# Modulation by rows with an accumulating multiply, and the gates' one-hot matrices in 16 bit with the tokens innermost

## The reference, cut to what matters

```python
c_act = jax.nn.silu(c)                                  # c: 1 x 2048
mod = (c_act @ w_ada[l] + b_ada[l]).reshape(B, 6, 1, D)  # w_ada: 2048 x 12288
shift1, scale1, gate1, shift2, scale2, gate2 = jnp.moveaxis(mod, 1, 0)
h = rmsnorm(x, g_norm_mix[l]) * (1.0 + scale1) + shift1
```

```python
s_half = jnp.einsum('thpd,hpkd->thpk', q, sub_keys)      # 128 keys on each of 2 sides
v_half, i_half = lax.top_k(s_half, K)                    # 16 best of each side, then 16 best pairs
a = jnp.einsum('cd,ced->ce', hc, w_u[ec])
coef = gc * jax.nn.gelu(a)                               # gate times activation
out = jnp.einsum('ce,ced->cd', coef, w_v[ec])
```

## Time and profile before

| | |
|---|---|
| runs, us | 3499.93, 3502.94, 3509.88 (median 3502.94) |
| profiled execution: span from the first to the last instruction, us | 3499.1 |
| around the span: median less span, us | 3.8 |
| busy: PE / DVE / ACT / POOL, us | 3167.9 / 2285.7 / 1244.0 / 155.9 |
| instructions | 51027 |

### The profile page before, as it was taken

The page is one execution under the profiler, slowest core; times in us unless marked ns, Lnnn a source line. Parts: engine busy times, 40 slices in busy tenths (PEclk is TensorE's granted clock), DMA queues, the critical chain, the costliest instruction groups (busy, mean ns, idle before and its releaser), DMA issues. The chain is left out here.

```text
span 3499.1 us, 51027 instructions
## 1 busy us (share of the span) xinstructions
PE 3167.9 (91%) x19812; PEld 2876.9 (82%) x19812; DVE 2285.7 (65%) x2591; ACT 1244.0 (36%) x1305; POOL 155.9 (4%) x240
## 2 busy tenths in 40 slices
PE   6999697998686999876799899999999999999997
PEld 5898476898575899865699899988899889988786
DVE  5674466674466666256637968854887468889844
ACT  4442343442333333032333333334333433333343
POOL 1010001010001100001000000000000000000000
PEclk9999898999898999578899999999999999999998
DMA  7764275764175777102544444455344554444453
GB/s 271 269 223 166 83 255 191 265 233 172 64 257 204 253 276 274 66 1 99 214 158 153 153 150 159 161 183 192 144 156 168 192 180 144 156 150 163 157 193 131
DMA packets 98853, 619.24 MB, mean 177 GB/s; under 512 B 10960, under 2 KB 11088, under 8 KB 35920
## 3 DMA queue, kind: packets, MB, share of 16 engines
q1 hardware_dynamic: 69968, 508.83, 40.7%
q0 software_dynamic: 28800, 109.25, 8.4%
HBM read 615.95 MB, written 2.10 MB: 177 GB/s over the span
## 5 line engine op out<-in xcount | busy, mean ns | idle before, releaser
L1238 DVE TENSOR_TENSOR wl<-ring,wh 128x2048 fp32r<-128x2048 f32 x468 | 1071.5, 2290 | 720.5 <-ACT wh L843 450.9
L843 ACT ACTIVATE wh<-ring 128x2048 fp32r<-128x2048 f32 x468 | 894.8, 1912 | 752.3 <-PE ps L427 305.6
L437 PE MATMUL ps<-hh,wh 128*128 128x256 f32 x3712 | 1068.7, 288 | 32.1 <-DVE wl L1238 23.3
L438 PE MATMUL ps<-hl,wh 128*128 128x256 f32 x3712 | 1057.1, 285 | 0.0
L439 PE MATMUL ps<-hh,wl 128*128 128x256 f32 x3712 | 1057.0, 285 | 0.0
L437 PEld LDWEIGHTS ps<-hh,wh 128*128 128x128 f32 x3712 | 719.5, 194 | 37.5 <-DVE wl L1238 28.2
L438 PEld LDWEIGHTS ps<-hl,wh 128*128 128x128 f32 x3712 | 720.0, 194 | 0.1
L439 PEld LDWEIGHTS ps<-hh,wl 128*128 128x128 f32 x3712 | 719.0, 194 | 0.0
L425 PE MATMUL ps<-wh,hh 128*128 128x512 f32 x864 | 342.8, 397 | 52.7 <-DVE hl L1231 27.7
L426 PE MATMUL ps<-wl,hh 128*128 128x512 f32 x864 | 338.9, 392 | 0.0
L427 PE MATMUL ps<-wh,hl 128*128 128x512 f32 x864 | 338.8, 392 | 0.0
(11 more groups left out here) (235 smaller groups left out, 3004.6 us busy)
## 6 DMA issues: line engine op xcount, KB each, us to landing
ring<-in_stream SPq DMA_DIRECT2D x480, 1024.0 KB, 4.8
aring<-in_ada POOLq DMA_DIRECT2D x192, 512.0 KB, 4.6
X<-in_x SPq DMA_DIRECT2D x1, 2048.0 KB, 11.7
BIG<-in_nbr_bias POOLq DMA_DIRECT2D x2, 1024.0 KB, 5.0
BIG<-in_g_post POOLq DMA_DIRECT2D x2, 1024.0 KB, 5.1
out<-X SPq DMA_DIRECT2D x2, 1024.0 KB, 4.0
BIG<-in_decays POOLq DMA_DIRECT2D x1, 1536.0 KB, 6.8
aring<-in_keys POOLq DMA_DIRECT2D x1, 1024.0 KB, 6.3
```

Of the source, the lines that this page charges most:

```text
L437: mm(o, wh[:, c % 2, w], hh[:, k, :], start=(k == 0), stop=False)
L438: mm(o, wh[:, c % 2, w], hl[:, k, :], start=False, stop=False)
L843: return nc.scalar.activation(o, i, func, **kw)
L1238: return tt(wl[:, c % 2, :], ring[:, c, :], wh[:, c % 2, :].bitcast(F32), ALU.subtract)
```

## The change

- The modulation weights are transposed on the host: each of the 192 units now holds 128 outputs on the partitions and half (1024) of the input rows. DVE does one instruction for a unit, a multiply by the row `crow` that writes its product back into `aring` and its sum into one column of `mod_parts`. `reduce_modulation` and its waits are gone from TensorE. `take_modulation` is two small additions on DVE, done three times in all: after both layers, in the third block after its column projections, and after its output projection.
- `crow` (silu of the condition, repeated on all partitions, 128 x 2048) replaces a column form of 128 x 16. It is loaded with a DMA of its own, issued by SP behind that of `X` and ahead of units 1 to 3 of the ring, and ACT's first `Silu` runs over all of it.
- `acc` is gone; the attention output `OT` takes the place of `PF`/`PF2` chunks, and the decay table is two tables, each with a DMA and a semaphore.
- `hot1`, `hot2`, `index`, the gate parts and an equality matrix are 16 bit with the 8 tokens innermost. The gate has three parts, built once after routing. A copy `iota8` of the key numbers, 8 times repeated, is made on DVE ahead of the routing. `hot2` has two buffers.
- A token's product is 128 x 96 and reads both operands with a step of 8 elements of 16 bit (16 bytes). A batch fills two PSUM banks. `gate_sum` reads 768 values for 512, `gsum` has two buffers, and `gated` runs over contiguous groups of 8 tokens. In a slot DVE now does all of the next batch ahead of the sum of this one.

```diff
-ADA_UNIT = 2 * 512
+ADA_UNIT = DM // 2
+MOD_CUTS = (0, 4 * A_TM2, 4 * A_WO2, 4 * ADA_CG)
...
-        hot1 = sb("hot1", [P, 2, BATCH, KEYS], F32R)
-        hot2 = sb("hot2", [P, BATCH, 2, PART], F32R)
-        gate_parts = sb("gate_parts", [P, 2, SEQ], F32R)
+        hot1 = sb("hot1", [P, 2, KEYS, BATCH], BF16)
+        hot2 = sb("hot2", [P, 2, GATE_PARTS, PART, BATCH], BF16)
+        equal2 = sb("equal2", [P, 2, PART, BATCH], BF16)
+        iota8 = sb("iota8", [P, KEYS, BATCH], BF16)
+        gate_parts = sb("gate_parts", [P, GATE_PARTS, SEQ], BF16)
...
+            sp.dma_start(crow, cond.rearrange("p (a b) -> p a b", a=2)).then_inc(cond_ready, 16)
             for s in range(1, R):
                 sp.dma_start(ring[:, s, :], stream[s]).then_inc(w_ready[s], 16)
...
-                pe.wait_ge(a_used, l * (ADA_LAYER * ADA_H) + ((ADA_TM + ADA_FM) * ADA_H + 2))
-                reduce_modulation(ADA_TM + ADA_FM, 4)
-                pe.wait_ge(mod_done, l * 2 + 1)
...
                 for j in range(BATCH):
-                    last = mm(ps[:, bank, j * 2 * PART:(j + 1) * 2 * PART], hot1[:, b, j, :],
-                              hot2[:, j, :, :].rearrange("p a b -> p (a b)"), start=True, stop=True)
+                    at = (j % 4) * TOKEN_COLS
+                    last = mm(ps[:, bank + j // 4, at:at + GATE_PARTS * PART], hot1[:, b, :, j],
+                              hot2[:, b, :, :, j].rearrange("p a b -> p (a b)"), start=True, stop=True)
...
-            f(csilu[:, :], small_of("cond"), ACT.Silu).then_inc(c_ready, 1)
+            act.wait_ge(cond_ready, 16)
+            f(crow, crow, ACT.Silu).then_inc(c_ready, 1)
...
-            def modulation(cg, h, i):
+            def modulation(cg, h):
                 dve.wait_ge(a_ready[h % 2], cg * 64 + 16 * (h // 2 + 1))
-                for kk in range(2):
...
-                        ins = stt(acc[:, i, :], w, csilu[:, k:k + 1], acc[:, i, :], ALU.mult, ALU.add)
-                    ins.then_inc(a_used if kk else a_step, 1)
+                u = cg * ADA_H + h
+                w = aring[:, h % 2, :]
+                stt(w, w, 1.0, crow[:, h % 2, :], ALU.mult, ALU.mult,
+                    accum_out=mod_parts[:, bass.ds(u, 1)]).then_inc(a_used, 1)
...
+            def take_modulation(part):
...
+                dve.wait_ge(a_used, 2 * end + 2)
+                tt(mod[:, cols], pair[:, :, 0], pair[:, :, 1], ALU.add).then_inc(mod_sum, 1)
+                dve.wait_ge(mod_sum, part + 1)
+                tt(mod[:, cols], mod[:, cols], small_of("b_ada")[:, cols], ALU.add).then_inc(mod_done, 1)
...
+            st(v.tensor_copy(iota8[:, :, :], small_of("iota").unsqueeze(2).to_broadcast([P, KEYS, BATCH])))
...
-            st(tt(gate_parts[:, 1, :], ps[:, 2, 0:SEQ], gate_parts[:, 0, :].bitcast(F32), ALU.subtract))
+            st(tt(gate_left, ps[:, 2, 0:SEQ], gate_parts[:, 0, :], ALU.subtract))
             st.done()
+            st(v.tensor_copy(gate_parts[:, 1, :], gate_left))
+            st.done()
+            st(tt(gate_parts[:, 2, :], gate_left, gate_parts[:, 1, :], ALU.subtract))
...
+                tt(hot1[:, b, :, :], token(index[:, 0, :], t0, KEYS), iota8[:, :, :], ALU.is_equal)
+            def hot_second(q, n, t0, b):
+                tt(equal2[:, b, :, :], token(index[:, 1, :], t0, PART), iota8[:, q * PART:(q + 1) * PART, :],
+                   ALU.is_equal).then_inc(hot_step, 1)
+                dve.wait_ge(hot_step, n + 1)
+                shape = [P, GATE_PARTS, PART, BATCH]
+                tt(hot2[:, b, :, :, :], equal2[:, b, :, :].unsqueeze(1).to_broadcast(shape),
+                   gate_parts[:, :, bass.ds(t0, BATCH)].unsqueeze(2).to_broadcast(shape), ALU.mult).then_inc(hot_done, 1)
...
+                src = ps[:, bank:bank + 2, :].rearrange("p k c -> p (k c)").rearrange("p (t s i) -> p i t s", t=BATCH, s=4)
+                v.tensor_reduce(gsum[b], src[:, :, :, 0:GATE_PARTS], AX, ALU.add).then_inc(sum_step, 1)
...
-                o = act_e[q % 2][:, :, bass.ds(t0, BATCH)].rearrange("p i t -> p t i")
-                tt(o, o, gsum, ALU.mult).then_inc(g_used, 1)
+                o = act_e[q % 2][:, :, bass.ds(t0, BATCH)]
+                tt(o, o, gsum[b], ALU.mult).then_inc(g_used, 1)
...
                 hot_first(t0 + BATCH, (c + 1) % 2)
-                gate_sum(n, bank + c % 2)
-                second_equal(q, t0 + BATCH)
-                gated(q, n, t0)
-                second_low(n + 1, t0 + BATCH)
-                second_high(n + 1, t0 + BATCH)
+                hot_second(q, n + 1, t0 + BATCH, (c + 1) % 2)
+                gate_sum(n, bank + apart * (c % 2), c % 2)
+                gated(q, n, t0, c % 2)
```

More of the change, by code:

```diff
@@ L154, with block @@
 DVE_STEPS, POOL_STEPS = 52, 7
-def block(nc, stream, ada, small, const1, const2, decays, keys, nbr_bias, g_post, g_final, x, out):
+HH = 4480
+WH = HH + 2 * KD * SEQ
+WL = WH + 2 * UNIT
+ACTS = WL + 2 * UNIT
+GATE_PARTS = 3
+TOKEN_COLS = 128
+def block(nc, stream, ada, cond, small, const1, const2, decays, keys, nbr_bias, g_post, g_final, x, out):
     ctx = ExitStack()
@@ L440, in up @@
                 last.then_inc(unit_done, 1)
[L442 to L448, removed]
             def prenorm(i):
@@ L746, in up_quarter @@
                         if q:
-                            batch(i * R + (b0 + c), c % 2, c % 2)
+                            batch(i * R + (b0 + c), c % 2, 2 * (c % 2))
                         up(i + g0, c, i * R + (n0 + c))
@@ L859, in prenorm, with halves, high_operand @@
                           bias=shift(k)).then_inc(ht_done, 1)
-            def high_operand(src):
+            def halves(src):
+                return [src[:, 0:8, :], src[:, 8:16, :]]
+            def high_operand(parts):
                 for half in range(2):
-                    k = slice(half * 8, half * 8 + 8)
-                    f(hh[:, k, :], src[:, k, :], ACT.Copy).then_inc(hh_done, 1)
+                    f(hh[:, half * 8:half * 8 + 8, :], parts[half], ACT.Copy).then_inc(hh_done, 1)
             def high(g, c, free=False):
@@ L1189, in _ @@
             pl.memset(kz, 0.0).then_inc(zeroed, 1)
-            pool.wait_ge(mod_done, 2 * LAYERS + 1)
-            pool.dma_start(area(0, DECAY_W), decays).then_inc(decay_ready, 16)
+            for i in range(2):
+                pool.dma_start(decay3[i].rearrange("p a b -> p (a b)"),
+                               decays[:, i * (DECAY_W // 2):(i + 1) * (DECAY_W // 2)]).then_inc(decay_ready[i], 16)
             pool.wait_ge(nss_done, 1)
@@ L1224, in prenorm, with halves, low_operand @@
                         ts(o, src, scale(k), shift(k), ALU.mult, ALU.add).then_inc(ht_done, 1)
-            def low_operand(src, use):
+            def halves(src):
+                return [src[:, 0:8, :], src[:, 8:16, :]]
+            def low_operand(parts, use):
                 for half in range(2):
@@ L1230, in low_operand @@
                     dve.wait_ge(hh_done, use * 2 + (half + 1))
-                    tt(hl[:, k, :], src[:, k, :], hh[:, k, :].bitcast(F32), ALU.subtract).then_inc(hl_done, 1)
+                    tt(hl[:, k, :], parts[half], hh[:, k, :].bitcast(F32), ALU.subtract).then_inc(hl_done, 1)
                 dve.wait_ge(hl_done, use * 2 + 2)
@@ L1241, in next_low @@
                 low(g + (c + 1) // R, (c + 1) % R).then_inc(lo_done, 1)
-            def modulation(cg, h, i):
+            def modulation(cg, h):
                 dve.wait_ge(a_ready[h % 2], cg * 64 + 16 * (h // 2 + 1))
-                for kk in range(2):
[L1247 to L1256, removed]
-                        ins = stt(acc[:, i, :], w, csilu[:, k:k + 1], acc[:, i, :], ALU.mult, ALU.add)
-                    ins.then_inc(a_used if kk else a_step, 1)
-            def take_modulation(count, n, cols, bank):
-                dve.wait_ge(mod_full, count)
-                tt(mod[:, cols], ps[:, bank, 0:4 * n], small_of("b_ada")[:, cols], ALU.add).then_inc(mod_done, 1)
+                u = cg * ADA_H + h
[3 more added lines that the diff above has]
+            def take_modulation(part):
+                first, end = MOD_CUTS[part], MOD_CUTS[part + 1]
+                cols = slice(first, end)
+                pair = mod_parts[:, 2 * first:2 * end].rearrange("p (a b) -> p a b", b=2)
+                dve.wait_ge(a_used, 2 * end + 2)
+                tt(mod[:, cols], pair[:, :, 0], pair[:, :, 1], ALU.add).then_inc(mod_sum, 1)
+                dve.wait_ge(mod_sum, part + 1)
+                tt(mod[:, cols], mod[:, cols], small_of("b_ada")[:, cols], ALU.add).then_inc(mod_done, 1)
             def rotate(dst, src, tmp, cos, sin, heads, half):
@@ L1455, in _ @@
             st.region(LAYERS * DVE_STEPS)
-            dve.wait_ge(mod_done, 2 * LAYERS)
+            take_modulation(0)
+            dve.wait_ge(mod_done, 1)
             def scales(a, j):
```

132 lines of the change are left out of this document (55 added, 77 removed).

## The result

The changed kernel takes 3536.3 us (median of 4 runs, 3531.3 to 3538.1) against 3502.2 for the kernel before beside it: a ratio of 1.0093, 95% interval 1.0079 to 1.0108. It is slower by 0.9%. Forecast was 3460, so the forecast was wrong, in sign too; what came is the direction of rival 2. The profiled execution spans 3533.0 us, 33.9 more than before's 3499.1.

What follows compares the result with a forecast made beforehand. TensorE was taken to bound the kernel, with DVE as full in V2. Modulation −20.4, gate products −16, DVE's relief −8 and +1.2 sum to −43.2 us, from 3502.9 to 3460 us; range 3420 to 3502.

Steps and rivals of the forecast that it cites:

- rival 2: Gate products on TensorE: the 16-byte step makes each dear, 187 ns, +79 us, 3558 us in all; chance 0.13.
- The modulation: All modulation steps together, from the start through the third block, with DVE's own cost: −20.4 us.
- +1.2 for `iota8` and the steps after routing: DVE's work ahead of routing (`iota8`) and small gate-part steps after it, against a cheaper first batch: +1.2 us.
- Start: Up to the first matmul: the `crow` load adds 2.5 us and the longer Silu 1.7; +4.2 us (0 to 7).
- Layers: Layers 0 and 1: sums over partitions and handshake gone, −13.7 us; 20 transposes faster in each, −3.2 us (0 to −5).
- Third block: Ahead of the compression matmuls: −5.5 us, not the 10.9 the sums take, since POOL's clearing is late next.
- at the output projection: Third block's output projection, DVE's multiply: gain 1.7 us less the new additions' remainder, −1.6 us.
- The gate products: 1024 products on TensorE at 95 ns each instead of 110: −16 us (ends −57 and +79).
- The two ends of that term: Price of a gate product: 54 ns from the stream of columns alone, 187 ns with DVE's 1.7-times step price.
- its relief: DVE's faster gated slots let TensorE keep its pace in V2 and shorten gaps: −8 us (0 to −13).
- That the products keep their price: Gate products stay at 110 to 135 ns because the weight load sets the pace: 3478 to 3503 us; chance 0.17.
- That DVE gains nothing from 16 bit: DVE then bounds V2 with a slot of 6.4 us and the lag stays: 3475 us; chance 0.12.

Runs made afterwards that it cites:

- x4_pairs: Changed kernel with keys innermost, gate-product operands contiguous 16-bit rows, each token's index and gate parts stored twice for VectorE; 3415.1 us, ratio 0.9738 to the kernel before.
- x3_modulation: Changed kernel's modulation with the gate products, one-hot matrices and single gate-sum buffer of the kernel before; 3484.2 us, ratio 0.9936 to the kernel before.
- x2_stepsize: Changed kernel, TensorE's gate operands 4 (U1), 8 (U2), 16 bytes apart with 64 columns (U3), contiguous in V2; sums wrong; 3438.5 us.
- x5_plain: As x4_pairs, but VectorE reads one stored copy of each token's index and gate part, held for the row of keys; 3458.2 us.

## Why the prediction was wrong, step by step

**The modulation: right, within what can be told.** Forecast −20.4 with everything up to the first batch; with +1.2 for `iota8` and the steps after routing, −19.2. Measured at U1's start: −20.7 in the changed kernel, −18.3 in x4_pairs and −15.9 in x3_modulation; by the medians of the runs −22 (−16 to −29) for the modulation alone. Its terms:
- Start: forecast +4.2, measured +5.2 (first row matmul 37.28; before it was at 32.1). The row landed by 15.65, 2.1 us after X before, for 2.5 forecast. The missing term is ACT's table load, 1.28 us, which now comes between landing and Silu; before it stood ahead of the wait (7.66 to 8.94 us).
- Layers: the sums over partitions and their handshake are gone, and the 20 transposes take 2.40 us. In layer 0 the score matmuls behind them, 5.2 us late at the start, come 3.1 us early: −8.3; in layer 1 11.9 early, so −8.8 more. 17.1 against 13.7 + 3.2 = 16.9.
- Third block: TensorE starts the compression at 1393.73 for 1413.51, 7.9 us more in hand than in layer 1. From the end of the column projections to the compression it is 11.4 us before (from 1402.09) and 5.9 after (from 1387.79): −5.5, as forecast, and POOL's clearing is what DVE waits for, as foretold. The other 2.4 us were gained ahead of that step, and no wait was found for them. From the compression to U1 come only 0.9 more (forecast −1.6, at the output projection).
- What these terms can be told from: U1's start varies by 4.8 us among kernels that are the same up to there but for the copy of the key numbers (2049.1 after, 2051.5 in x4_pairs, 2053.9 in x3_modulation, which has no copy and is last). So the +1.2 was not seen, and part of the −20.7 goes with the clock and not with a wait: one less the granted clock, summed over windows of 10 us from 320 to 2050, comes to 155 us in the changed kernel, 161 in x4_pairs, 162 in x3_modulation and 163 before.

**The gate products: here it failed.** The term "I take 95, near today's row, since the weight load has the same 128 columns and something of a step's price will be paid" was −16 us; it measured 179 ns, so 96 x 0.54 + 32 x 0.52 = +69. The two ends of that term were good: contiguous, a product costs 50 ns (54 foretold from the stream of columns), and with the step 179 (187 foretold from the price of `gated`'s step). That the upper end fits is luck: it took 1.7 times on all 110 ns of an fp32r product of 64 columns, where the runs show about four times on each of 96 bf16 columns, 3.6 times the contiguous product. The error was to put the value between the ends, near a row that was neither: the fp32r product's 110 ns foretold neither the 50 nor the 179. Smaller steps do cost less (92 ns at 8 bytes), but this kernel has 16 bytes in all 128 batches. The place of the 16 bytes was known, and rival 2 had it with its price, at a chance of 0.13 that was far too low. What spoke for it was already in the trace, that a large step cost DVE 1.7 times; what I held against it (that step is 64 times wider) was no reason, since here 16 bytes do it as well.

The Trainium skill, "Advanced Engine Details and Errata", section "SBUF Cachelines", was right in direction: with a step of 16 bytes no 16-byte line is hit twice, and the product is dear. It isn't right in its threshold for TensorE: at 8 bytes a line is still hit twice, and the column already costs 0.81 ns for 0.41 (x2_stepsize, both operands stepped). Here the measurement decides: 4 bytes are free, 8 bytes cost double.

**DVE: right in each duration; its relief can't be read off cleanly.** All five instructions came as forecast (the second comparison took 284 ns). The relief was put at −8 (0 to −13). What is left between the price of the longer products and the growth of the stages is 54.5 − 69 = −14. In U1 there is none (+17.1, for 32 x 0.54). In U2, U3 and V2, TensorE's idle time falls from 4.5, 7.7 and 5.5 us to 2.0, 4.2 and 2.9 (stage length less busy time above), 8.6 together. The low clock behind those gaps shrinks too: one less the granted clock, summed over windows of 5 us, comes to 13.6 us before and 6.6 after in these three stages, which is enough for the rest. But the −14 is not the relief that was priced: TensorE's slots became 0.54 us longer, which gives DVE more room in each by itself; no run parts the two. In x4_pairs, where they are 0.5 us shorter than before, the stages shrink by 66.5 us and the slots account for some 62 of them (96 x 0.48 + 32 x 0.49), so about −5 is left, and TensorE's idle time in the three stages (4.7, 7.0 and 5.5 us) is hardly below before's. Two of TensorE's waits, answering to the earlier trace rows: for `hot` it falls from 14.6 us, for `wl` ahead of column products it stays (23.3 before):

```profile
PE ps L450 <- DVE wl L1239: 24.2, 20, 3.0
...
PE ps L728 <- DVE hot L1750: 6.7, 2, 4.0
```

**The other rivals.** That the products keep their price is refuted from both sides: with the same weight load of 128 columns one costs 50 ns contiguous and 179 with the step. That DVE gains nothing from 16 bit is refuted for this change, but it isn't idle: x5_plain is a kernel in which it is true.

## What to carry to other kernels

A layout that serves the engine that writes a tile is paid for by the engine that reads it. Before turning the innermost dimension, write down the byte step of every reader, and if one of them is TensorE's moving operand and sits on the path, keep it at 4 bytes or less; two adjacent 16-bit elements were all that DVE needed, and TensorE read them at no cost. And where a cost has two ends that stem from two mechanisms (here: the stream of columns sets the pace, or the step does), don't forecast the middle: choose a mechanism, and give the other its full chance.

## What the runs showed of the hardware that was not expected

- TensorE's moving operand in bf16, at 2.4 GHz: about 0.4 ns a column when contiguous or 4 bytes apart, 0.81 at 8 bytes and 1.72 at 16 bytes with the stationary operand stepped too; stepped alone at 16 bytes, 1.63 (170 − 14 over 96). The stationary operand 16 bytes apart costs 26 ns for a load of 128 columns when nothing else is stepped (76 for 50 ns), and 9 ns beside a stepped moving one (179 for 170).
- DVE's pace in 16 bit hangs on the innermost dimension of its inputs: 1024 elements take 684 ns when it is two adjacent stored elements, and 1218 ns when the input is one element held (step 0).
- A bf16 product of 96 columns, weights included, takes 50 ns, and an fp32r one of 64 columns 110 ns.
- The table load ahead of a Silu and the one behind it take 1.28 us each, and it stands on the path where the Silu comes between two other functions right at the start.
